# Two-block transformer kernel: buffers moved to multiples of 2048 bytes, and the first two output tiles of each down and mixing projection interleaved

## The reference

```python
def first_block(x, ...):                      # 2 layers
    for l in range(DEPTH):
        u = rmsnorm(x, norm_mix[l])
        proj = u @ w_in[l]                    # q, k, v, indexer, convolution, gates
        ...
        y_attn = dsa_attention(q, k, v, iq, ik, iw) @ w_attn_out[l]
        y_conv = (cB * short_conv(cC * ch, conv_w[l])) @ w_conv_out[l]
        merged = gates[:, :, 0] * y_attn + gates[:, :, 1] * y_conv
        x = x + merged @ w_mix_out[l]         # the mixing projection
        u = rmsnorm(x, norm_mlp[l])
        x = x + jnp.square(jax.nn.relu(u @ w_mlp_up[l])) @ w_mlp_down[l]   # up, down
    return rmsnorm(x, norm_final)

def second_block(x, c, ...):                  # 1 layer
    mod = jax.nn.silu(c) @ w_ada[l] + b_ada[l]
    ...
    x = x + gt_m[:, None, :] * token_mixer(...)
    x = x + gt_f[:, None, :] * swiglu(h, w_gate[l], w_up[l], w_down[l])
```

## Time and profile before

| | us |
|---|---|
| median of 3 runs | 2298.73 (2297.31 to 2299.01) |
| the profiled execution | 2293.53 |
| its span | 2291.7 |
| PE busy | 2211.3 (96%) |
| DVE busy | 1020.1 (45%) |
| POOL busy | 932.5 (41%) |
| ACT busy | 686.2 (30%) |
| mean granted TensorE clock | 0.982 of full speed |

### The profile page before, as it was taken

How to read it: one execution, slowest core, us unless ns; L and a number is a source line. 1 busy time by engine, 2 the same in 40 slices (tenths; PEclk the granted TensorE clock), 3 DMA queues, 4 the chain that set the end, 5 groups by cost and what they waited for, 6 DMA issues and landing times. The chain is left out here.

```text
span 2291.7 us, 27490 instructions
## 1 busy us (share of the span) xinstructions
PE 2211.3 (96%) x10008; PEld 1760.4 (77%) x10008; DVE 1020.1 (45%) x1645; ACT 686.2 (30%) x910; POOL 932.5 (41%) x712
## 2 busy tenths in 40 slices
PE   7999999999999999999999999996999998999999
PEld 5787777888888768777778888875967676888887
DVE  3575324555464736823346455476154333111111
ACT  4123443322222312244332212233254323212221
POOL 3453233445444444432344445432332213444444
PEclk9999999999999999999999999997999988999999
DMA  4222112233333322221123333331221102222222
GB/s 167 91 97 83 65 56 92 99 141 128 129 128 110 130 91 101 92 71 58 61 105 134 123 129 128 128 128 68 74 71 59 55 5 88 92 92 94 103 97 92
DMA packets 35235, 220.98 MB, mean 96 GB/s; under 512 B 5172, under 2 KB 5556, under 8 KB 9400
## 3 DMA queue, kind: packets, MB, share of 16 engines
q1 hardware_dynamic: 27696, 189.80, 23.6%
q10 hardware_dynamic: 7432, 29.74, 3.9%
HBM read 214.54 MB, written 2.10 MB: 95 GB/s over the span
## 5 line engine op out<-in xcount | busy, mean ns | idle before, releaser
L304 POOL TENSOR_TENSOR w_lo<-w_raw,w_hi 128x512 fp32r<-128x512 f32 x708 | 932.3, 1347 | 1346.1 <-ACT w_hi L730 1346.1
L321 PE MATMUL ps<-a_hi,w_hi 128*128 128x512 f32 (+1 forms) x1600 | 631.0, 394 | 1.5 <-POOL w_lo L304 1.5
L323 PE MATMUL ps<-a_hi,w_lo 128*128 128x512 f32 (+1 forms) x1600 | 623.8, 390 | 0.0
L322 PE MATMUL ps<-a_lo,w_hi 128*128 128x512 f32 (+1 forms) x1600 | 623.6, 390 | 0.0
L730 ACT ACTIVATE w_hi<-w_raw 128x2048 fp32r<-128x2048 f32 x177 | 339.1, 1916 | 877.6 <-PE ps L323 851.1
L321 PEld LDWEIGHTS ps<-a_hi,w_hi 128*128 128x128 f32 (+1 forms) x1600 | 297.4, 186 | 87.1 <-issue 22.0
L323 PEld LDWEIGHTS ps<-a_hi,w_lo 128*128 128x128 f32 (+1 forms) x1600 | 297.3, 186 | 66.9
L322 PEld LDWEIGHTS ps<-a_lo,w_hi 128*128 128x128 f32 (+1 forms) x1600 | 297.7, 186 | 63.7
L321 PE MATMUL ps<-b_hi,w_hi 128*128 128x512 f32 x816 | 326.3, 400 | 4.6 <-POOL w_lo L304 2.4
L322 PE MATMUL ps<-b_lo,w_hi 128*128 128x512 f32 x816 | 323.3, 396 | 0.0
L323 PE MATMUL ps<-b_hi,w_lo 128*128 128x512 f32 x816 | 323.2, 396 | 0.0
(11 more groups left out here) (236 smaller groups left out, 2241.7 us busy)
## 6 DMA issues: line engine op xcount, KB each, us to landing
w_raw<-in_weights SPq DMA_DIRECT2D x177, 1024.0 KB, 4.8
v<-in_ada ACTq DMA_DIRECT2D x24, 1024.0 KB, 4.8
x<-in_x_in SPq DMA_DIRECT2D x2, 1024.0 KB, 11.3
out<-x SPq DMA_DIRECT2D x8, 256.0 KB, 2.0
bias<-in_mult_bias ACTq DMA_DIRECT2D x1, 640.0 KB
cs_rope<-in_rope ACTq DMA_DIRECT2D x1, 512.0 KB, 8.3
g<-q ACTq DMA_DIRECT2D x16, 32.0 KB, 2.1
g<-k ACTq DMA_DIRECT2D x16, 32.0 KB, 2.0
```

The costliest lines, as they stand in the source:

```text
L304: last = nc.gpsimd.tensor_tensor(w_lo[:, s, piece], w_raw[:, s, piece], f32(w_hi[:, s, piece]), ALU.subtract)
L321: nc.tensor.matmul(o, wh, hi(kt), start=kt == 0, stop=False)
L322: nc.tensor.matmul(o, wh, lo(kt), start=False, stop=False)
L323: last = nc.tensor.matmul(o, wl, hi(kt), start=False, stop=kt == depth - 1)
```

## The change

Three things are changed. A padding buffer `front` of 1920 bytes is put ahead of `x`, and the small buffers and `bias` are moved behind the large ones, so that each operand of the large matmuls starts at a multiple of 2048 bytes: `x` 18432, `a_hi` 34816, `a_lo` 51200, `w_hi` 83968, `w_lo` 100352, `y_hi` 124928, `y_lo` 133120, `b_hi` and `q` 188416, `k` 196608, `b_lo` 204800, `bias` 221184. `iw_rows` becomes the second row of `mrows`. And the first two tiles of each mixing projection (2 places), of each down part of a chunk (8) and of each down group of the second block (3) are computed as a `tile_pair`.

```diff
+ROW, FIRST_FREE = 4 * S, 16512
...
+        sb("front", [P, (ROW - FIRST_FREE % ROW) // 4])
         x = sb("x", [P, KT, S])
...
-        bias = sb("bias", [P, TRI[TT]])
...
-        iw_rows = sb("iw_rows", [IDX_HEADS, S])
...
+        one.enter_context(nc.sbuf_tensor("region_1", [P, 2 * KT * S], F32))
+        ctx.enter_context(one)
+
+        bias = sb("bias", [P, TRI[TT]])
...
-            def tile_pair(o, s, src, ready, depth=KT):
+            def tile_pair(o, s, src, ready, depth=KT, deep=None):
...
+                        if j == B_MIX:
+                            for u in range(2):
+                                pe.wait_ge(bank_free[(t + u) % 4], nth(L, LAYER_TILES // 4, (t + u) // 4))
+                            tile_pair([ps[(t + u) % 4][:, :] for u in range(2)], s, src,
+                                      lambda kt: pe.wait_ge(merged_split, nth(L, KT, kt)))
+                            continue
...
+                        if b == 4:
+                            for u in range(2):
+                                pe.wait_ge(bank_free[u], nth(L, LAYER_TILES // 4, c * 4 + (first_tile(B_MLP) + 8) // 4))
+                            tile_pair((ps[0][:, :], ps[1][:, :]), 0, (b_hi, b_lo),
+                                      lambda kt: pe.wait_ge(h_split, nth(L, 8 * CHUNKS, c * 8 + kt)))
+                            continue
...
-                            if n == 8:
-                                def ready(kt):
-                                    pe.wait_ge(h_split, nth(L, 8 * CHUNKS, c * 8 + kt))
...
+                    if b == 0:
+                        for u in range(2):
+                            pe.wait_ge(bank_free[(2 * j + u) % 4], nth(L, LAYER_TILES // 4, (2 * j + u) // 4))
+                        tile_pair([ps[(2 * j + u) % 4][:, :] for u in range(2)], j % 2, (b_hi, b_lo),
+                                  lambda kt: pe.wait_ge(h_split, nth(L, 8 * CHUNKS, hid + kt)), depth=nt, deep=KT)
+                        j += 1
+                        continue
```

More of the change, by code:

```diff
@@ L127, in two_blocks @@
         ctx.enter_context(one)
+        bias = sb("bias", [P, TRI[TT]])
+        rms_col = sb("rms_col", [P, 3 * TT])
+        lp = sb("lp", [P, LP_N])
+        sp = sb("sp", [P, SP_N])
+        mod = sb("mod", [P, 48])
+        gs = sb("gs", [P, 2 * KT])
+        cs = sb("cs", [P, KT])
+        iw = sb("iw", [P, TT, IDX_HEADS])
+        top = sb("top", [P, 3, 8])
+        peak = sb("peak", [P, 4 * TT])
+        warm = sb("warm", [P, 1])
+        nudge = sb("nudge", [P, 1])
+        acol = sb("acol", [P, 2, TT, MH])
+        qcol = sb("qcol", [P, 3, 32])
+        mcol = sb("mcol", [P, 4, MH, TT])
         ps = [ctx.enter_context(nc.psum_tensor(f"ps{b}", [P, S], F32)) for b in range(8)]
@@ L314, in _, with product @@
         def _(pe):
-            def product(o, s, deep, depth, c0, m, hi, lo, ready=None):
+            def product(o, s, deep, depth, c0, m, hi, lo):
                 for kt in range(depth):
-                    if ready is not None:
-                        ready(kt)
                     wh, wl = wcols(w_hi, s, deep, kt, c0, m), wcols(w_lo, s, deep, kt, c0, m)
@@ L324, in product, with tile @@
                 last.then_inc(tile_done, 1)
-            def tile(L, t, s, deep, c0, hi, lo, m=P, depth=None, ready=None):
+            def tile(L, t, s, deep, c0, hi, lo, m=P, depth=None):
                 pe.wait_ge(bank_free[t % 4], nth(L, LAYER_TILES // 4, t // 4))
                 product(ps[t % 4][0:m, :], s, deep, depth or deep, c0, m,
-                        lambda kt: hi[:, kt, :], lambda kt: lo[:, kt, :], ready)
-            def tile_pair(o, s, src, ready, depth=KT):
+                        lambda kt: hi[:, kt, :], lambda kt: lo[:, kt, :])
+            def tile_pair(o, s, src, ready, depth=KT, deep=None):
                 for kt in range(depth):
@@ L335, in tile_pair @@
                     for u in range(len(o)):
-                        wh, wl = wcols(w_hi, s, depth, kt, u * P, P), wcols(w_lo, s, depth, kt, u * P, P)
+                        wh, wl = (wcols(w, s, deep or depth, kt, u * P, P) for w in (w_hi, w_lo))
                         nc.tensor.matmul(o[u], wh, src[0][:, kt, :], start=kt == 0, stop=False)
@@ L480, in _ @@
                             continue
-                        for u in range(2):
-                            ready = None
-                            if j == B_MIX and u == 0:
-                                def ready(kt):
-                                    pe.wait_ge(merged_split, nth(L, KT, kt))
-                            tile(L, t + u, s, KT, u * P, *src, ready=ready)
+                        if j == B_MIX:
[4 more added lines that the diff above has]
+                            continue
+                        for u in range(2):
+                            tile(L, t + u, s, KT, u * P, *src)
                             if j < B_YATT:
@@ L714, in _ @@
                     pe.wait_ge(w_lo_ready, nth(L, LAYER_BLOCKS, j))
-                    for u in range(2):
[L716 to L720, removed]
+                    if b == 0:
[5 more added lines that the diff above has]
+                        continue
+                    for u in range(2):
+                        tile(L, 2 * j + u, j % 2, KT, u * P, b_hi, b_lo, depth=nt)
                     j += 1
```

8 lines of the change are left out of this document (3 added, 5 removed).

## The result

| us | before | after |
|---|---|---|
| median of 5 runs | 2298.7 (2292.97 to 2299.01) | 2285.32 (2281.75 to 2285.6) |
| profiled execution | 2293.53 | 2285.2 |
| its span | 2291.7 | 2283.4 |
| mean granted clock of the profiled execution | 0.982 | 0.983 |
| mean granted clock of runs at the median's time | 0.981 | 0.983 |

The ratio is 0.9943, with the interval 0.9932 to 0.9954: 13.4 us faster, at least 10.6 and at most 15.6. The forecast was 2295.7, a time that counts as no difference (0.36 in all, where "faster" had 0.39). The result lies in the range (2280 to 2311), between the forecast and the rival "no wait after tile 10" (2281), although that wait did come.

What follows compares the result with a forecast made beforehand. PE, busy 96% of the span with its clock granted nearly throughout, was taken as the bound. The terms -16.3 - 3.0 + 16.3 gave -3.0 us, so 2295.7 us against the median 2298.73, range 2280 to 2311 (0.81).

Steps and rivals of the forecast that it cites:

- no wait after tile 10: MLP chunks: DVE gets through sooner than counted, so PE does not wait there; 2281 us in all, chance 0.12.
- Part 1: Addresses: matmuls on `b` lose 6.7 ns each, 2448 of them, and become like `a`, which stays unchanged; 16.3 us less.
- what `b` has of its own is that it starts 32 bytes past a multiple of 64: Matmuls on `b`: this offset was taken as the cause of 233.3 ns against 226.7 for `a`.
- The other rival of this part, that `b` is slow because it lies high: Matmuls on `b`, above byte 195,000: the offset is not the cause, `b` keeps 233 ns; 2311 us, chance 0.10.
- crossing 2048 bytes is free: Moving operands: rows of `a` that cross a multiple of 2048 bytes pay nothing for it, so `a` gains nothing.
- The rival that every float32r matmul loses its surcharge: All float32r matmuls: 9 ns less for about 5,600 and 16 ns less for 2448; about 2231 us, chance 0.07.
- the two matmuls of 1.02 us in the earlier trace: Plain float32 matmuls reading `q` and `k`, taken as two clocks a column with some 4 ns of surcharge.
- Part 2: Waits the pairs take away: 2.3 us in the mixing projections and 0.7 in the second block's third group; 3.0 us less.
- Part 3: Waits the pairs bring in the MLP chunks, as tile 8 ends later and DVE starts later: 16.3 us more.
- The six middle chunks: Chunks not last of their layer: PE waits 1.5 us after tile 10 for DVE's reduction, six times; 9.2 us more.
- The last chunk of layer 1: DVE is full and starts 4.6 us late; PE's waits grow and one likely lowers the clock; 4.6 us more.
- Layer 2: Its last chunk: DVE starts late as well, but the clock already fell here before; 2.5 us more.

Runs made afterwards that it cites:

- the first three experiments: Against the kernel before: new addresses with old tile order, 2278.81 us; pairs at old addresses, 2300.5; the change without pairs in the eight MLP chunks, 2274.51.
- the fifth: The changed kernel without pairs in the MLP chunks and with the small matmuls after tiles 11, 13 and 15: 2268.66 us, ratio 0.9874 to the kernel before.

## Why the prediction was right and wrong

**Part 1, size right, reason wrong.** Forecast -16.3. A tile of `b` takes 0.16 us less, as said; over all 2,360 or so distances of `b` at full clock and without a wait, those between tiles with them, the mean fell from 233.3 to 227.1 ns, 6.2 ns, so 2448 of them give -15.2. `a` stayed unchanged, as said. But the step "what `b` has of its own is that it starts 32 bytes past a multiple of 64" failed: with every operand there, nothing was slow, and with `a` at a multiple of 2048 and the weights 32 off, `a` was. I compared two moving operands and looked at their addresses only. The weights are read too, at the other end of the same instruction, and the numbers were in the list of addresses. That the size came out is luck in this sense: the edit made both the offset and the distance equal, so it would have come out by either reason.

The other rival of this part, that `b` is slow because it lies high, fell as well: it lies highest after the change too and is fast. The earlier trace rows were rightly read: crossing 2048 bytes is free, and the kernel at 128 past such multiples shows it directly. The rival that every float32r matmul loses its surcharge did not come: 226.7 ns remain at every good distance. The rule of the Trainium skill that I weighed for it ("TensorE: Matmul & The Clock Gate", "Back-to-back issue gap", 216 ns for a single warm gap of 512 columns) is reached in no kernel here. One reading was off without touching the sum: the two matmuls of 1.02 us in the earlier trace rows are one float32 matmul of the kernel, which PE runs as two instructions (line 374 has 24 matmuls of 512 columns, the trace 48), so plain float32 takes four clocks a column, not two.

**Part 2, right.** Forecast -3.0; the gaps that went are 1.06 twice and 0.59, so -2.7, and with the slower restarts beside them, which the forecast had counted in, -3.2. The wait at the head of the mixing projection stayed.

**Part 3, right in its chain, a little too dear.** The eight gaps are 1.30, where I had 1.5 and 1.4. The six middle chunks cost 7.8 (forecast 9.2). The last chunk of layer 1: 1.30, plus 0.50 on the second wait, less 0.51 for the third that no longer comes (I had 1 to 2 there), plus 3.4 for 6.8 us at half clock: 4.7 (forecast 4.6). That these two agree is partly luck: the forecast had the waits growing by some 4 us and the clock as likely, and the waits grew by 1.3. Layer 2: 1.30 + 0.51 = 1.8 (forecast 2.5). Together +14.3, forecast +16.3. The shorter multiplication was the right choice (2.29 us, forecast 2.3). POOL's split is beside its last 0.43 us and costs it nothing; in the kernel before, where a split was under way when the multiplication began, it took 2.64, 2.77 and 3.07 us with 0.49, 0.63 and 0.92 us of split beside it. Step by step the change is thus -15.2 - 3.2 + 14.3 = -4.1, and by the stages of the table -3.7.

**What the sum did not have.** Measured were -13.4. They come apart so: -3.7 in the stages that the change touches, -4.6 in the others, and -5.1 because the profiled execution before stood 5.2 us below its median and that of the changed kernel 0.1 below its own. The last two are mostly the clock. Of 28 other runs of the kernel before, the twelve with a mean clock of 0.981 took 2298.07 to 2299.36, the four with 0.983 or more 2289.64 to 2292.77: the same program, 5 to 10 us apart. (Against the median of these 28, 2297.3, the change is worth 12 us.) I carried the 5.2 us over to the changed kernel as a constant, and there they were 0.1. Time by clock is a rough test: 2298.7 x 0.981 = 2255.0 and 2285.3 x 0.983 = 2246.5, 8.5 less (rounding leaves up to 2.3 to either side). The steps without their 3.4 us of clock give -7.5. So the work was forecast well; of the 13.4 us some 5, with as much rounding, are a higher mean clock, where the sum of the steps has 3.4 us of a lower one. In the trace 3.5 us of it come from the second block's mixer, which the change doesn't touch. Why the half-clock stretches fall otherwise there isn't shown: among the experiments they lie differently again, in kernels whose code for that stage is the same.

That is also why the forecast stood at "same" and the result is a clear gain: 0.2% is 4.6 us, and the uncertainty of the clock, about as large, stood in no term and no bound. That the result lies in the range is owed to the rival of 2281 that set its lower end, whose mechanism did not come.

## What to carry to other kernels

Compare the distance of two starts over all pairs of operands: where one group of otherwise equal matmuls is slower by a few ns, look at the distance between the weights and the moving operand before the address of either, and keep it at a multiple of 256 bytes; here it is worth 6.7 ns of 233 per matmul. That is measured for float32r with 512 moving columns and offsets of 32, 64 and 128 bytes; other types and offsets were not tried. Interleaving two tiles delays the first tile's end by nearly a whole tile, so it pays only where PE waits for its input, and costs where an engine behind that tile is the next thing PE waits for. And before you add steps of a few us to a profiled execution, see how its mean clock stands among the runs, and compare the clock in stages that the change doesn't touch.

## What the runs showed of the hardware that I had not expected

- The rate of a float32r matmul depends on the distance of the two operands in SBUF, 226.7 ns against 233.3 at 512 columns, and with the roles turned round 120 against 117 to 119 at 256 columns: a distance bad for the one is good for the other. All these numbers are at full clock.
- A float32r matmul on `a` pays 13.4 ns over its 213.3 ns of columns at every good distance, whatever multiple of 2048, 128 or 32 bytes it starts at.
- How long PE waits doesn't alone decide on the clock. The eight gaps of 1.30 us left it at full speed. Of eleven gaps of 2.8 to 3.3 us at the end of the layers (two each in the kernel before, the change, and the first three experiments, one in the fifth), three had no half-clock stretch behind them, two had one of 3.4 us and six one of 6.8 us, and a gap of 3.18 is among the three. Two more of 3.2 us, in the kernel with the weights 32 bytes off, left the clock at full speed too.
